# Token sums on one column, a spread of rstd by TensorE, filler products, and odd tiles' h_lo on GpSimd

## What is computed

```python
def rms_norm(x, g):
    y = xf * rsqrt(mean(xf * xf, axis=-1, keepdims=True) + EPS)
    return y * g
# first block
h = rms_norm(x, norm_mix);  x = x + mix(h @ w_in) @ w_out        # attention and a linear recurrence
x = x + conv_ffn(rms_norm(x, norm_ffn))
# second block, two layers; h*(1+scale)+shift, scale and shift from c @ mod_w
modulate(h, shift, scale) = h * (1 + scale) + shift
...
x = x + gate * 0.5 * swiglu(modulate(rms_norm(x, g0), ...))
x = x + gate * mixer(modulate(rms_norm(x, g1), ...))              # layer 0 pooling, layer 1 attention
x = x + gate * 0.5 * swiglu(modulate(rms_norm(x, g2), ...))
out = rms_norm(x, final_g)
```

## Time and profile before

| | us |
|---|---|
| median of 3 runs | 3148.03 (3146.73 to 3151.39) |
| profiled execution | 3149.93 |
| its span | 3148.2 |
| TensorE busy | 2941.6 |
| VectorE busy | 1546.6 |
| ScalarE busy | 983.8 |
| GpSimd busy | 143.3 |

### The profile page before, as it was taken

One profiled execution on the slowest core, in us unless ns is written; L12 is line 12 of the kernel. 1 busy time (PEld: TensorE's weight loads), 2 busy tenths in 40 slices (PEclk: granted clock), 3 DMA queues, 4 the chain that ended last, 5 costly groups with the idle time before them and its releaser, 6 DMA issues.

```text
span 3148.2 us, 35103 instructions
## 1 busy us (share of the span) xinstructions
PE 2941.6 (93%) x13383; PEld 2304.6 (73%) x13383; DVE 1546.6 (49%) x2189; ACT 983.8 (31%) x1520; POOL 143.3 (5%) x201
## 2 busy tenths in 40 slices
PE   7989888889999999999978999999999999899998
PEld 5844767778778876888856888778877863778876
DVE  5355655446677745555454332243324469343322
ACT  3334334323333323222223222232222226332222
POOL 0000000001100011100110000000000000000000
PEclk9679988879999999999988999999999999899999
DMA  6101400027622254555612323322332220122331
GB/s 227 48 1 37 161 1 1 1 77 227 198 87 94 92 167 142 194 193 197 179 46 81 99 94 93 96 86 93 98 92 84 94 67 1 48 86 93 98 92 64
DMA packets 89885, 309.09 MB, mean 98 GB/s; under 512 B 10288, under 2 KB 14000, under 8 KB 89648
## 3 DMA queue, kind: packets, MB, share of 16 engines
q1 hardware_dynamic: 69040, 232.07, 22.9%
q0 software_dynamic: 20736, 75.51, 7.5%
HBM read 305.44 MB, written 2.10 MB: 98 GB/s over the span
## 4 chain that ended last, share of the span: by engine, by line
PE 87%; DVE 9%; ACT 2%; issue 1%; DMA 0%; SPq 0%; POOL 0%; DVEq 0%; ACTq 0%
PE psum L1646 24%; PE psum L1647 23%; PE psum L1648 23%; PE psum L1843 1%; PE psum L1980 1%; PE psum L1986 1%; PE psum L1831 1%; DVE rexp L953 1%; PE psum L1694 1%; PE psum L1783 1%; PE psum L1690 1%; PE psum L1691 1%; DVE nmax L1581 1%; PE psum L1659 1%; PE psum L2158 1%
## 5 line engine op out<-in xcount | busy, mean ns | idle before, releaser
L947 DVE TENSOR_TENSOR w_lo<-stage,w_hi 128x1024 fp32r<-128x1024 f32 (+3 forms) x445 | 519.5, 1167 | 856.4 <-ACT w_hi L543 856.3
L1646 PE MATMUL psum<-h_hi,w_hi 128*128 128x512 f32 x2248 | 889.2, 396 | 18.5 <-POOL h_lo L526 14.7
L1647 PE MATMUL psum<-h_lo,w_hi 128*128 128x512 f32 x2248 | 878.1, 391 | 0.0
L1648 PE MATMUL psum<-h_hi,w_lo 128*128 128x512 f32 x2248 | 877.9, 391 | 0.0
L543 ACT ACTIVATE w_hi<-stage 128x1024 fp32r<-128x1024 f32 (+3 forms) x445 | 450.5, 1012 | 1295.2 <-PE psum L1648 1271.5
L1646 PEld LDWEIGHTS psum<-h_hi,w_hi 128*128 128x128 f32 x2248 | 423.8, 189 | 116.5 <-POOL h_lo L526 15.5
L1647 PEld LDWEIGHTS psum<-h_lo,w_hi 128*128 128x128 f32 x2248 | 423.7, 188 | 93.1 <-issue 5.5
L1648 PEld LDWEIGHTS psum<-h_hi,w_lo 128*128 128x128 f32 x2248 | 423.3, 188 | 89.0
L1646 PE MATMUL psum<-hid_hi,w_hi 128*128 128x512 f32 x880 | 349.1, 397 | 6.5 <-DVE hid L1032 6.5
L1647 PE MATMUL psum<-hid_lo,w_hi 128*128 128x512 f32 x880 | 348.8, 396 | 0.0
L1648 PE MATMUL psum<-hid_hi,w_lo 128*128 128x512 f32 x880 | 348.6, 396 | 0.0
(11 more groups left out here) (364 smaller groups left out, 2819.7 us busy)
## 6 DMA issues: line engine op xcount, KB each, us to landing
stage<-in_up SPq DMA_DIRECT2D x220, 512.0 KB, 3.5
mod_w<-in_mod_w POOLq DMA_DIRECT2D x144, 512.0 KB, 4.2
...
```

The costliest lines, as they stand in the source:

```text
L947: dve.tensor_tensor(w_lo[:, c % 2, 0:kt * cols], stage[:, c % NSTAGE, 0:kt * cols], w_hi[:, c % 2, 0:kt * cols].bitcast(F32), ALU.subtract ...
L1646: pe.matmul(dst, wh[:, n], a_hi[:, k], start=start and n == 0, stop=False)
L1647: pe.matmul(dst, wh[:, n], a_lo[:, k], start=False, stop=False)
L1648: m = pe.matmul(dst, wl[:, n], a_hi[:, k], start=False, stop=stop and n == kt - 1)
```

## The change

- **Sums.** `sum_squares` uses the squares as weights, 128 tokens at a time, and one column of `means` as the moving operand: four matmuls of one column. The result is four columns with the tokens on the partitions.
- **Root and reciprocal** then work on 128x4 (`std`, `rstd`).
- **Spread.** `spread_rstd` on TensorE brings `rstd` back to a row on all partitions, in PSUM bank 5, by four matmuls of 128 columns with a column of `rstd` repeated as weights. t is computed with that PSUM row as an operand.
- **Fillers.** `keep_busy` are matmuls into bank 7 that nothing reads: 512 columns behind the sum of `sq_sum`, 256 behind the last sum, twice 512 behind the spread, at the norms in `POOLED` alone.
- **Buffers.** t has four buffers, `norm_t` and the two halves of `rexp`.
- **GpSimd.** `h_lo` of odd tiles is made by GpSimd (`low_parts`) from t and `h_hi`. Where there is a shift, ScalarE first adds it to t in place, waits for its own result, and then copies it to `h_hi`. VectorE makes the even tiles.
- **Padding.** Two unused tensors of `APART` = 376 columns move the overlaid tensors.

```diff
+        turn_t = [norm_t[:, 0], norm_t[:, 1]] + [rexp[:, n].rearrange("p t n -> p (t n)") for n in range(2)]
+
+        def h_lo_ready(eng, n_norm, k):
+            norms = [n for n in range(n_norm) if n != 3]
+            if n_norm == 3 or k % 2:
+                before = (KD // 2) * len(norms) + KD * (n_norm > 3)
+                eng.wait_ge(hlo_pool, before + (k + 1 if n_norm == 3 else k // 2 + 1))
+            else:
+                eng.wait_ge(hlo_done, (KD // 2) * len(norms) + k // 2 + 1)
...
+            def low_parts(n_norm):
+                for k in range(1, KD, 2):
+                    pool.wait_ge(hhi_done, KD * NORM[n_norm] + k + 1)
+                    pool.tensor_tensor(h_lo[:, k], turn_t[k % 4], h_hi[:, k].bitcast(F32),
+                                       ALU.subtract).then_inc(hlo_pool, 1)
...
-                act.activation(rstd, psum[:, 4, :], ACT.Sqrt, bias=eps[:, 0:1]).then_inc(std_done, 1)
+                act.activation(std[:], psum[:, 4, 0:TT], ACT.Sqrt, bias=eps[:, 0:1]).then_inc(std_done, 1)
...
-                    act.activation(h_hi[:, k], norm_t[:, k % 2], ACT.Identity, bias=shift(k)).then_inc(hhi_done, 1)
+                    if k % 2 and n_norm > 1:
+                        act.activation(turn_t[k % 4], turn_t[k % 4], ACT.Identity, bias=shift(k)).then_inc(shifted, 1)
+                        shifts[0] += 1
+                        act.wait_ge(shifted, shifts[0])
+                        act.activation(h_hi[:, k], turn_t[k % 4], ACT.Copy).then_inc(hhi_done, 1)
+                    else:
+                        act.activation(h_hi[:, k], turn_t[k % 4], ACT.Identity, bias=shift(k)).then_inc(hhi_done, 1)
...
-                dve.reciprocal(rstd, rstd).then_inc(rstd_done, 1)
-                dve.wait_ge(rstd_done, NORM[n_norm] + 1)
+                dve.reciprocal(rstd[:], std[:]).then_inc(rstd_done, 1)
+                dve.wait_ge(rbc_done, NORM[n_norm] + 1)
...
-                        if k >= 2:
-                            dve.wait_ge(hlo_done, base + k - 1)
-                        dve.scalar_tensor_tensor(out=norm_t[:, k % 2], in0=xT[:, k], scalar=scale(k),
-                                                 in1=rstd, op0=ALU.mult, op1=ALU.mult).then_inc(t_done, 1)
-                    if k >= 1:
+                        if k >= 4:
+                            h_lo_ready(dve, n_norm, k - 4)
+                        dve.scalar_tensor_tensor(out=turn_t[k % 4], in0=xT[:, k], scalar=scale(k),
+                                                 in1=psum[:, 5, :], op0=ALU.mult, op1=ALU.mult).then_inc(t_done, 1)
+                    if k % 2:
...
+            def keep_busy(count):
+                for cols in count:
+                    pe.matmul(psum[:, 7, 0:cols], ident, cst[:, 0:cols], start=True, stop=True)
+
             def sum_squares(n_norm, k):
+                def over_tokens(src, start, stop):
+                    for tt in range(TT):
+                        m = pe.matmul(psum[:, 4, tt:tt + 1], src[:, tt * P:(tt + 1) * P], means[:, 0:1],
+                                      start=start and tt == 0, stop=stop, skip_group_check=True)
+                    return m
...
                     pe.wait_ge(acc_done, adds_before(n_norm) + ADDS)
-                    pe.matmul(psum[:, 4, :], means, sq_sum, start=True, stop=False)
+                    over_tokens(sq_sum, True, False)
+                    keep_busy([512])
                 pe.wait_ge(sq_done, KD * NORM[n_norm] + k + 1)
-                pe.matmul(psum[:, 4, :], means, sq(n_norm, k), start=k == 0, stop=k == KD - 1).then_inc(ssq_done, 1)
+                over_tokens(sq(n_norm, k), first, k == KD - 1).then_inc(ssq_done, 1)
+                if n_norm in POOLED:
+                    keep_busy([256])
+
+            def spread_rstd(n_norm):
+                pe.wait_ge(rstd_done, NORM[n_norm] + 1)
+                for tt in range(TT):
+                    m = pe.matmul(psum[:, 5, tt * P:(tt + 1) * P], rstd[:, tt:tt + 1].to_broadcast([P, P]), ident,
+                                  start=True, stop=True)
+                m.then_inc(rbc_done, 1)
+                if n_norm in POOLED:
+                    keep_busy([512, 512])
```

More of the change, by code:

```diff
@@ L33 @@
 LAG = 3
+APART = 376
 NSTAGE = 4
@@ L172, in build @@
         norm_t = sb("norm_t", [P, 2, S])
+        std = sb("std", [P, TT])
         warm_out = sb("warm_out", [P, 1])
+        rstd = sb("rstd", [P, TT])
         rexp = sb("rexp", [P, 2, TT, P])
@@ L218, in build @@
         rstd_done = sem("rstd_done")
+        rbc_done = sem("rbc_done")
         t_done = sem("t_done")
@@ L221, in build @@
         hlo_done = sem("hlo_done")
+        hlo_pool = sem("hlo_pool")
+        shifted = sem("shifted")
         silu_done = sem("silu_done")
@@ L320, in build @@
             lmask = mask8[:, 2 * P:].rearrange("p (l n) -> p l n", l=6)
-            o_hi, o_lo, y_hi, y_lo = mixer_phase(
-                ("o_hi", [P, KD, S], F32R), ("o_lo", [P, KD, S], F32R), ("y_hi", [P, KD, S], F32R),
+            _, o_hi, o_lo, y_hi, y_lo = mixer_phase(
+                ("apart_mix", [P, APART], F32), ("o_hi", [P, KD, S], F32R), ("o_lo", [P, KD, S], F32R), ("y_hi", [P, KD, S], F32R),
                 ("y_lo", [P, KD, S], F32R))
@@ L326, in build @@
             mixer.close()
-        rstd, sq_sum = [rexp[:, n].rearrange("p t n -> p (t n)") for n in range(2)]
+        sq_sum = rexp[:, 1].rearrange("p t n -> p (t n)")
         x_tok, = phase(("x_tok", [P, TT, D], F32))
-        hid_hi, hid_lo, s_buf, hid, taps = phase(
-            ("hid_hi", [P, KF, S], F32R), ("hid_lo", [P, KF, S], F32R),
+        _, hid_hi, hid_lo, s_buf, hid, taps = phase(
+            ("apart_ffn", [P, APART], F32), ("hid_hi", [P, KF, S], F32R), ("hid_lo", [P, KF, S], F32R),
             ("s_buf", [P, 2, S], F32), ("hid", [P, 2, S], F32), ("taps", [P, 2, S], F32))
@@ L506, in _ @@
             mod_loads(0, 2)
+            low_parts(0)
             mod_loop(2, 58)
@@ L512, in _ @@
                 gather(1, n)
+            low_parts(1)
             for n in range(KD):
@@ L516, in _ @@
                 gather(2, n)
+            low_parts(2)
             mod_loads(87, 88)
@@ L526, in _ @@
                 pool.tensor_tensor(h_lo[:, k], diff[:, k // 2 % 2, k % 2], h_hi[:, k].bitcast(F32),
-                                   ALU.subtract).then_inc(hlo_done, 1)
-            for n_norm in (5, 6, 7, 8):
+                                   ALU.subtract).then_inc(hlo_pool, 1)
+            low_parts(4)
+            for n_norm in (5, 6, 7):
                 gather_all(n_norm)
+                low_parts(n_norm)
+            gather_all(8)
         @block.scalar
@@ L963, in norm @@
                     if k < KD:
-                        if k >= 2:
-                            dve.wait_ge(hlo_done, base + k - 1)
-                        dve.scalar_tensor_tensor(out=norm_t[:, k % 2], in0=xT[:, k], scalar=scale(k),
-                                                 in1=rstd, op0=ALU.mult, op1=ALU.mult).then_inc(t_done, 1)
-                    if k >= 1:
+                        if k >= 4:
[3 more added lines that the diff above has]
+                    if k % 2:
                         dve.wait_ge(hhi_done, base + k)
-                        dve.scalar_tensor_tensor(out=h_lo[:, k - 1], in0=norm_t[:, (k - 1) % 2], scalar=shift(k - 1),
+                        dve.scalar_tensor_tensor(out=h_lo[:, k - 1], in0=turn_t[(k - 1) % 4], scalar=shift(k - 1),
                                                  in1=h_hi[:, k - 1].bitcast(F32), op0=ALU.add,
@@ L1649, in product @@
                 m.then_inc(unit_done, 1)
+            def keep_busy(count):
+                for cols in count:
+                    pe.matmul(psum[:, 7, 0:cols], ident, cst[:, 0:cols], start=True, stop=True)
             def sum_squares(n_norm, k):
+                def over_tokens(src, start, stop):
[3 more added lines that the diff above has]
+                    return m
+                first = k == 0
                 if n_norm in POOLED:
@@ L1655, in sum_squares @@
                         return
+                    first = False
                     pe.wait_ge(acc_done, adds_before(n_norm) + ADDS)
-                    pe.matmul(psum[:, 4, :], means, sq_sum, start=True, stop=False)
+                    over_tokens(sq_sum, True, False)
+                    keep_busy([512])
                 pe.wait_ge(sq_done, KD * NORM[n_norm] + k + 1)
-                pe.matmul(psum[:, 4, :], means, sq(n_norm, k), start=k == 0, stop=k == KD - 1).then_inc(ssq_done, 1)
+                over_tokens(sq(n_norm, k), first, k == KD - 1).then_inc(ssq_done, 1)
[9 more added lines that the diff above has]
+                    keep_busy([512, 512])
             def up(f, n_norm):
@@ L1733, in _ @@
             if first_block:
+                spread_rstd(0)
                 s = seg["mix_in"]
@@ L2088, in _ @@
                 mixed_out("mix_out", 1, y_unit)
+                spread_rstd(1)
                 up(0, 1)
@@ L2105, in _ @@
```

(5 more changed lines are left out.)

15 lines of the change are left out of this document (8 added, 7 removed).

## The result

| | before | after |
|---|---|---|
| median (lowest to highest), us | 3149.71 (3146.73 to 3156.54), 4 runs | 3110.03 (3106.82 to 3111.41), 4 runs |
| ratio, 95% interval | | 0.987, 0.9851 to 0.9888 |
| profiled execution, its span, us | 3149.93, 3148.2 | 3111.41, 3109.7 |

The change makes the kernel 39.7 us faster. The sign was right; nearly half of the gain comes from something to which I had given no microsecond. One execution of the kernel before, beside experiments 1 to 4, took 4905.1 us at a mean granted clock of 0.552; it is left out of every comparison.

What follows compares the result with a forecast made beforehand. TensorE, busy 93% of the span, was taken as the bound, so only its standstills at the nine norms counted. Savings at heads and loops, less 1.3 at norm 0, summed to 20.0 us: 3128 us, range 3119 to 3141.

Steps and rivals of the forecast that it cites:

- The step that failed: Claim that what moves on other queues costs nothing and the padding `APART` adds no instruction: 0 us.
- The head: At each norm, from the end of the last square to the first normed tile: 2.85 us against 5.40, 2.55 saved.
- The clock in the head: Between squares and first products, fillers hold TensorE's granted clock near 1, against 0.68 and 0.50 before.
- The rival (10 us): The clock falls in the head despite fillers, 0.8 on sum and 0.85 on spread at six heads: 3138 us, chance 0.16.
- Norm 1: First norm with fillers: 0.65 us lost to the filler between the sums; head saves 1.9, loop 0.8.
- Norm 0: Norm without fillers, one-column sums over eight tiles: 11.2 us against 7.60, 3.6 lost; together 1.3 lost.
- The loop: Eight tiles behind each head, up to the next unit: 0.3 to 0.4 us saved per loop, 0.8 at norms 0 and 1.
- its own bound behind tile 3: In the loop after tile 3's `h_lo`, TensorE's products set the time: 8.79 us for 37, where starts alone take 8.45.
- Norms 3, 4 and 8: Savings forecast: 4.6 us over norm 3, pool stage and norm 4; 2.8 us from norm 8 to the end.
- The shared port: Rival: VectorE's `h_lo` and GpSimd's wait for each other in every pair of tiles: 3163 us, chance 0.04.

Runs made afterwards that it cites:

- experiments 1 to 4: Padding tests: the change without padding, 3132.29 us; the kernel before with only 392 or 8 columns of padding, 3130.97 and 3132.49 us; TensorE products alone at various addresses.
- e1_no_pad: The change without the padding `APART`, everything else kept: median 3132.29 us, ratio to before 0.9944.
- e9_after_again: The changed kernel itself, unaltered, run once more for comparison on one chip: median 3109.79 us, ratio to before 0.9867.
- experiment 5: The change without its filler products (`keep_busy` issues nothing): median 3116.10 us.
- experiment 6: The change with every `h_lo` of the norms but norm 3 on VectorE again, without the shifted copy: median 3114.01 us.
- experiment 8: The change with `LAG` = 0 in place of 3, so the second unit's products of a tile follow at once on the first's: 3124.93 us.
- e2_before_pad392: The kernel before with nothing but a padding of 392 columns ahead of `hid_hi` and of `o_hi`: median 3130.97 us, ratio 0.9951.

## Why the prediction was wrong, point by point

- **The step that failed** is the last sentence of the sum: "the padding `APART` adds no instruction", so it costs nothing. It adds none, and moves the moving operand of 3024 products by 32 bytes within 64, against the weights. That is 17.2 us in the feed-forward stages; the experiments put it at 15.1 to 16.6 alone, and at 22.5 by the medians of `e1_no_pad` and `e9_after_again`, which ran on two different chips. The span fell by 18.5 us more than forecast, so this is nearly the whole of the miss. I had looked at moved instructions and never asked what else a tensor's place can change, although two groups of the page differed by 6 ns for no visible reason.
- **The head**, 2.55 saved: 2.46 at norm 2. Right in each part but the sum, which took 0.11 more than counted.
- **The clock in the head**: 1.00, as forecast, and experiment 5 shows that the fillers are the cause, at norms 2, 5, 6 and 7. The rival (10 us) would have been 6, since at norms 1, 3 and 8 the spread runs at the high clock without them.
- **Norm 1**: 0.65 lost by the filler, measured 0.84; the stretch -2.80 against -2.7. Two errors cancel here, which is luck: the head saved 1.61 where I had 1.9, and the loop 1.18 (15.49 to 14.31) where I had 0.8.
- **Norm 0**: "three tiles at 0.89 and five at 1.70" was wrong. All eight took 1.70, since the clock was low from the first pass. The sums lost 6.0 instead of 3.6, and the norm 3.4 instead of 1.3.
- **The loop**: size somewhat low (0.5 to 0.7 at each of norms 2, 4, 5, 6 and 7, I had 0.3 to 0.4), cause wrong. I gave it to the split; experiment 6 shows the split at zero or a little below. Tile 3 by GpSimd was placed well (6.56, measured 6.46). I also took TensorE to be its own bound behind tile 3; `w_lo` of the third unit runs just ahead of it, as experiment 8 shows.
- **Norms 3, 4 and 8**: -4.9 and -2.7 against -4.6 and -2.8.
- **The shared port** was rightly rated low. VectorE's `h_lo` next to GpSimd's took 0.95 at 1240.85 in place of 0.75, and at most 1.02 anywhere in the kernel; I had feared over 1.2, and had counted a delay of 0.4. The Trainium skill, page "SBUF — State Buffer", section "Who interferes with whom", has the two exclude one another; by that rule, the trace agrees, and as forecast the delay fell on even tiles, which set nothing.
- Not forecast and not explained: 1.5 us less in the attention stage (2.1 in `e1_no_pad`, 0.3 in `e2_before_pad392`, so not from the padding).
